# Order of ScalarE's and VectorE's work in RWKV's r stage, and the send of X by column halves, in a six-layer model on one core

## What is computed

```python
r, k, v = rkv[:, :, 0], rkv[:, :, 1], rkv[:, :, 2]
kk = heads(k * k_k)
kk = kk * lax.rsqrt(jnp.maximum(jnp.sum(kk * kk, axis=-1, keepdims=True), 1e-24))
k = k.astype(f32) * (1.0 + (a - 1.0) * k_a)

def step(state, inp):
    r_t, w_t, k_t, v_t, kk_t, a_t = inp
    sa = jnp.einsum('bhvk,bhk->bhv', state, kk_t)
    state = (state * w_t[:, :, None, :]
             - sa[..., None] * (kk_t * a_t)[:, :, None, :]
             + v_t[..., None] * k_t[:, :, None, :])
    return state, jnp.einsum('bhvk,bhk->bhv', state, r_t)
```

```python
y = jnp.einsum('bse,ed->bsd', jnp.concatenate([o_a, o_b], axis=-1), w_out)
y = rms_norm_2(y, post_g)
return x + gate[:, None, :] * y
```

## Time and profile before

| | |
|---|---|
| median of 3 runs | 2015.63 us (2000.81 to 2020.76) |
| the profiled execution | 2018.37 us |
| its span in the profile | 2016.6 us |
| TensorE busy | 1871.5 us (93%) |
| VectorE busy | 1301.9 us (65%) |
| ScalarE busy | 1037.8 us (51%) |
| GpSimd busy | 167.2 us (8%) |
| chain that ended last, on TensorE | 84% |
| mean granted clock | 0.957 |

### The profile page before, as it was taken

One profiled execution on the slowest core, in us unless ns is written; L12 is line 12 of the kernel. 1 busy time (PEld: TensorE's weight loads), 2 busy tenths in 40 slices (PEclk: granted clock), 3 DMA queues, 4 the chain that ended last, 5 costly groups with the idle time before them and its releaser, 6 DMA issues.

```text
span 2016.6 us, 43368 instructions
## 1 busy us (share of the span) xinstructions
PE 1871.5 (93%) x18631; PEld 1653.5 (82%) x18631; DVE 1301.9 (65%) x1838; ACT 1037.8 (51%) x1571; POOL 167.2 (8%) x124
## 2 busy tenths in 40 slices
PE   6988899999899999899799998987999999997997
PEld 6877698899767988898588887877778888886886
DVE  7775367855543777557657766777267765775764
ACT  5744365554333655445465544934365544564454
POOL 0051000000010000012100000042000000001000
PEclk8999999999887999999899999999989999997998
DMA  6320245556653555444547563320055555442541
GB/s 186 126 79 4 65 150 193 186 187 195 208 168 105 188 189 178 147 156 151 184 138 208 193 193 120 105 78 25 4 167 184 192 178 165 144 134 93 162 128 61
DMA packets 288262, 288.16 MB, mean 143 GB/s; under 512 B 15224, under 2 KB 286312, under 8 KB 288072
## 3 DMA queue, kind: packets, MB, share of 16 engines
q1 hardware_dynamic: 284776, 284.28, 44.2%
q10 hardware_dynamic: 3296, 1.11, 0.3%
HBM read 284.32 MB, written 1.05 MB: 142 GB/s over the span
## 4 chain that ended last, share of the span: by engine, by line
PE 84%; DVE 6%; issue 4%; ACT 4%; DMA 1%; POOL 0%; SPq 0%; DVEq 0%; ACTq 0%; POOLq 0%
PE ps L409 21%; PE ps L410 11%; PE ps L391 9%; PE ps L392 9%; PE ps L393 9%; PE ps L783 2%; PE ps L427 2%; PE ps L426 2%; PE ps L428 2%; PE ps L753 1%; PE ps L681 1%; ACT wh L443 1%; DVE wl L453 1%; PE ps L767 1%; PE ps L696 1%
## 5 line engine op out<-in xcount | busy, mean ns | idle before, releaser
L453 DVE TENSOR_TENSOR wl<-raw,wh 128x1024 fp32r<-128x1024 f32 x484 | 596.6, 1249 | 342.6 <-ACT wh L443 337.0
L443 ACT ACTIVATE wh<-raw 128x1024 fp32r<-128x1024 f32 x484 | 500.3, 1042 | 434.5 <-PE ps L410 197.2
L409 PE MATMUL ps<-HH,wh 128*128 128x512 f32 x1408 | 489.3, 391 | 0.0
L410 PE MATMUL ps<-HH,wl 128*128 128x256 f32 x1408 | 397.0, 282 | 0.0
L409 PEld LDWEIGHTS ps<-HH,wh 128*128 128x128 f32 x1408 | 264.3, 188 | 55.3
L391 PE MATMUL ps<-HH,wh 128*128 128x256 f32 x928 | 271.2, 292 | 12.8 <-DVE HH L2414 6.7
L410 PEld LDWEIGHTS ps<-HH,wl 128*128 128x128 f32 x1408 | 266.1, 189 | 0.1
L392 PE MATMUL ps<-HH,wh 128*128 128x256 f32 x928 | 263.6, 284 | 0.0
L393 PE MATMUL ps<-HH,wl 128*128 128x256 f32 x928 | 263.4, 284 | 0.0
L391 PEld LDWEIGHTS ps<-HH,wh 128*128 128x128 f32 x928 | 179.2, 193 | 23.5 <-issue 7.4
L391 PE MATMUL ps<-XH,wh 128*128 128x256 f32 x576 | 168.3, 292 | 16.0 <-DVE XH L1970 16.0
(11 more groups left out here) (328 smaller groups left out, 3256.0 us busy)
## 6 DMA issues: line engine op xcount, KB each, us to landing
raw<-in_ffn_w_gu_dram SPq DMA_DIRECT2D x88, 1024.0 KB, 5.1
raw<-in_ffn_w_down_dram SPq DMA_DIRECT2D x32, 1024.0 KB, 5.3
raw<-in_w_in_dram SPq DMA_DIRECT2D x32, 1024.0 KB, 5.5
raw<-in_rw_w_rkv_dram SPq DMA_DIRECT2D x24, 1024.0 KB, 5.9
B<-in_w_ada_dram SPq DMA_DIRECT2D x24, 1024.0 KB, 7.3
raw<-in_ds_w_in_dram SPq DMA_DIRECT2D x14, 1024.0 KB, 5.0
raw<-in_ffn_w_down_dram SPq DMA_DIRECT2D x16, 768.0 KB, 4.6
raw<-in_sb_w_qkv_dram SPq DMA_DIRECT2D x12, 1024.0 KB, 5.2
```

The source lines that it names most:

```text
L409: e.matmul(o[:, m, :], h_[:, k, c], x_, start=k0 + k == 0, stop=False, skip_group_check=True)
L410: i = e.matmul(o[:, m, 0:S], l_[:, k, c], x_[:, 0, :], start=False, stop=k0 + k == kt - 1, skip_group_check=True)
L443: e.activation(wh[:, u % UNITS, 0:kn * 256], raw[:, j % RAW, k0 * 256:(k0 + kn) * 256], ACT.Copy).then_inc(*up("hi"))
L453: e.tensor_tensor(wl[:, u % UNITS, 0:kn * 256], raw[:, j % RAW, k0 * 256:(k0 + kn) * 256], wh[:, u % UNITS, 0:kn * 256].bitcast(F32), ALU. ...
```

## The change

Three edits.

- The r stage of both RWKV layers. ScalarE now takes a key norm and one group's rounding of v's input in turn, four times; then come the change of table and both exponentials; the two weight roundings and the eviction of r's first block follow behind these. VectorE's two pairs of rests stand behind `erase_and_write(0)` and `erase_and_write(1)`, no longer ahead of them.
- At the end of both hybrid layers VectorE scales group g + 1 before it adds group g, and an addition waits for its own group's scaling alone.
- The last barrier is gone. TensorE's transposes are grouped by feature group, both token halves of one in one bank, and each waits for its own group of X; ScalarE copies a bank at once; SyncE sends columns 0 to 511 after the second copy and columns 512 to 1023 after the fourth.

```diff
@@ sync_program
-            e.wait_ge(*at("act", "x out"))
-            e.dma_start(out_ap.rearrange("a (j p) c -> p (a j) c", p=P), TM(0)).then_inc(s_out, 16)
-            e.wait_ge(s_out, 16)
+            for a in range(2):
+                c = slice(512 * a, 512 * a + 512)
+                e.wait_ge(*at("act", ("end", 2 * a + 1)))
+                e.dma_start(out_ap.rearrange("a (j p) c -> p (a j) c", p=P)[:, :, c], TM(0)[:, :, c]).then_inc(s_out, 16)
+            e.wait_ge(s_out, 32)
@@ tensor_program
-            barrier(e, "mm", "end")
-            for g in range(2):
+            for g in range(4):
+                o = bank(e, ("end", g), ("act", ("end", g)))
+                e.wait_ge(*at("dve", ("y", 1, g)))
                 for j in range(2):
-                    o = bank(e, ("end", g, j), ("act", ("end", g, j)))
-                    for u in range(4):
-                        i = e.transpose(o[:, u * P:u * P + P], X[:, 4 * g + u, j * P:j * P + P], ident)
-                    i.then_inc(*up("mm", ("end", g, j)))
+                    for u in range(2):
+                        i = e.transpose(o[:, (2 * j + u) * P:(2 * j + u) * P + P], X[:, 2 * g + u, j * P:j * P + P], ident)
+                i.then_inc(*up("mm", ("end", g)))
@@ act_rwkv
-            for g in range(3):
+            for g in range(4):
                 key_norm(g)
-            prepare(2, HH, ("unit", ("full", n, 1, 3)))
-            hi(e)
-            evac(0, 0, R_)
-            key_norm(3)
+                rounded(2, HH, g, ("unit", ("full", n, 1, 3)))
             log_and_exp(e)
             key_norm_exp(0)
             key_norm_exp(1)
+            hi(e)
+            evac(0, 0, R_)
@@ dve_rwkv
-            lo(e)
             erase_and_write(0)
             lo(e)
             erase_and_write(1)
+            lo(e)
@@ dve_hybrid
-            for g in range(4):
+
+            def y_normed(g):
                 for k in (2 * g, 2 * g + 1):
                     i = e.scalar_tensor_tensor(out=y[:, k, :], in0=y[:, k, :], scalar=gp[:, k:k + 1], in1=rstd[:, :], op0=ALU.mult, op1=ALU.mult)
-                i.then_inc(*up("dve"))
+                i.then_inc(*up("dve", (L, "yn", g)))
+
+            y_normed(0)
+            for g in range(4):
+                if g < 3:
+                    y_normed(g + 1)
                 xs = X[:, 2 * g:2 * g + 2, :]
-                e.wait_ge(*now("dve"))
+                e.wait_ge(*at("dve", (L, "yn", g)))
                 e.tensor_tensor(xs, xs, y[:, 2 * g:2 * g + 2, :], ALU.add).then_inc(*up("dve", ("y", layer, g)))
```

More of the change, by code:

```diff
@@ L1420, in act_rwkv, with rounded, prepare @@
             R_, k_, v_, cum, a_, vmix, kk, sq = FM(4), FM(5), FM(13), FM(7), FM(8), FM(14), FM(9), FM(6)
-            def prepare(m, hi_, *free):
+            def rounded(m, hi_, g, *free):
+                for ev in free:
+                    e.wait_ge(*at(*ev))
+                e.wait_ge(*at("dve", ("xm", n, m, g)))
+                e.activation(pair(hi_, g), mix_slot(g), ACT.Copy).then_inc(*up("act", ("xmh", n, m, g)))
+            def prepare(m, hi_):
                 for g in range(4):
[L1424 to L1427, removed]
+                    rounded(m, hi_, g)
             def evac(m, g, dst):
@@ L1878, in scalar_program @@
             act_hybrid(e, 1)
-            barrier(e, "act", "end")
             xo = TM(0)
[L1881 to L1884, removed]
+            for g in range(4):
+                e.wait_ge(*at("mm", ("end", g)))
+                e.activation(xo[:, :, g * 256:g * 256 + 256], PS("end", g)[:, :].rearrange("p (j c) -> p j c", j=2),
+                             ACT.Copy).then_inc(*up("act", ("end", g)))
         MX, NM, SM, RS = ([small[:, o + 8 * i:o + 2 + 8 * i] for i in range(4)] + [small[:, z:z + 2]]
@@ L2650, in vector_program @@
             dve_hybrid(e, 1)
-            barrier(e, "dve", "end")
         def pool_square(e, tag):
@@ L2757, in gpsimd_program @@
             pool_hybrid(e, 1)
-            barrier(e, "pool", "end")
         def begin(rehearsal):
```

## The result

| | before | after |
|---|---|---|
| median of 20 runs | 2005.42 us (1999.56 to 2021.12, and one of 2350.37) | 1995.07 us (1990.42 to 2008.5) |
| ratio | | 0.9945 (95% interval 0.9927 to 0.9963) |
| span of the profiled execution | 2016.6 us | 1992.3 us |

The ratio leaves out the one slow run of 2350.37 us. It is worth 11 us of 2005, with 7.4 to 14.6 us inside the interval. The forecast was a gain of 10.4 us. It was put under the median of three runs, 2015.63; twenty runs of the kernel before have a median 10 us lower, 2005.42. The changed kernel came out at 1995.07, under the low end of the range, 1996. It is faster, by less than 1%.

A forecast was written before the change was run, and what follows sets the result against it. TensorE was taken to bound the kernel; 3.4 (layer 0) + 3.1 (layer 3) + 4.2 (tail) - 0.3 (hybrid layer 0) = 10.4 us gained, giving 2008.0 profiled, 2005.2 at the runs' median, stated as 2006 us; range 1996 to 2014.

The forecast's parts named there:

- It lies 2.7 us over the median of the runs, 2015.63; that gives 2005.2: Whole kernel: forecast 2008.0 us for the profiled execution, lowered by 2.7 us to the level of the three runs' median.
- case c: Whole kernel: half-clock spells do not come up again at their shifted places, 10 us more gained, 1995 us; chance 0.13.
- ScalarE: RWKV r stage: ScalarE no longer waits between roundings, and the exponentials start near 77.3 instead of 82.06.
- VectorE: RWKV r stage: key halves start near 78.4, the second is ready at 90.3 instead of 95.2, TensorE's wait gone.
- the 1.2 us: r stage, layer 0: margin by which the rests of r's third group come before TensorE wants them, thinnest in the change.
- the data are there at 96.6, and the rest shifts by 3.4 us: Layer 0's grams: after an instruction refill the work resumes at 96.6 instead of 99.98, gaining 3.4 us, bounds 2.2 to 4.5.
- case (b): r stage: late rests or longer refills leave each layer 0 to 1 us; 5 us gained in all, 2011 us; chance 0.13.
- rival (a): Layer 0's grams: TensorE's clock falls to half after the new stop, costing 12 us; 1.6 us slower, 2017; chance 0.10.
- 84 records in a microsecond: Layer 0's grams: full-clock rate taken from layer 3, used to put the refill boundary, record 100, at 93.1 us.
- Layer 3: Layer 3's grams: VectorE wait of 3.10 us removed, first refill stop grows from 1.21 to 2.0 us, gain 3.1 us.
- The end: Last 15 us: earlier transposes by group give 2.95 us, the halved last send 1.3 us; 4.2 us in all, 2.8 to 5.0.
- If VectorE is first, nothing is lost: End of hybrid layer 0: GpSimd's first sum meets VectorE's third; 0.6 us lost if GpSimd is first; 0.3 us taken.

## Why the prediction was right or wrong

**The level, which put the time outside the range.** The step that failed is "It lies 2.7 us over the median of the runs, 2015.63; that gives 2005.2". Three runs were taken as the level, although they spread over 20 us. Twenty runs gave 2005.42. The forecast gain of 10.4 us taken off that is 1995.0, and 1995.07 was measured. Luck had a part in it: beside the experiments the same kernel's medians were 2010.79, 2012.32 and 2008.99 us, and the changed kernel's, in its second set of runs, was 1998.14, inside the range. The prediction did name half-clock stretches as the thing that moves a run by 12 us (case c, and the earlier trace rows), but it did not ask whether the execution profiled before, with a stretch of 24 us at 0.51, was one of the long ones, and whether three runs could give the level. Its range is also added up wrongly at one end: with the lowest bound of each term, 2.2, 2.3, 2.8 and -0.7, the least gain is 6.6 us, not 7.4.

**ScalarE.** Right in each step: exponentials near 77.3 (77.22), no wait between the roundings.

**VectorE.** Right: first half at 78.4 (78.40), second ready at 90.3 (90.31), the third block's rests in time, no wait of TensorE on either. The experiment with VectorE's order alone showed what stood behind the 1.2 us: 3.6 and 3.7 us of wait in the two layers, and the clock besides.

**Layer 0.** The step that failed is "the data are there at 96.6, and the rest shifts by 3.4 us". The boundary and the record of the stop were right (227, and the added matmuls moved it as that reading says). The length was not: 2.51 instead of 2.0 us, because the load of the next weight piece, which the moved rests now release later, runs beside the fetch. The prediction had seen that loads "now start later fall on the grams", in case (b), and had priced it at nothing in the sum. And the clock fell behind the stop. The sum had the grams at full clock; rival (a) had named a fall at this very place, and held layer 3's example against it. Of the 3.4 us, 0.8 were left in the profiled execution; in six other executions with the same r stage it was 0.6, 1.0, 1.2, 2.2, 2.2 and 2.6, the last three being those in which the clock stayed. A smaller error is the rate: the prediction reads 84 records in a microsecond as 84 records a microsecond, but that count takes in records that only overlap it; 160 records in 2.56 us are 63 a microsecond, which puts the boundary some 0.3 us later.

**Layer 3.** Right: 3.1 forecast, 3.0 measured, 3.0 to 3.3 in four of the other executions, and 1.5 and 1.2 in two, which have a half-clock stretch there. Its first stop was 1.49 instead of 2.0 us.

**The end.** Right: 4.2 forecast, 4.0 measured; 2.8 of it (2.95) by groups and 1.3 (1.3) by the smaller last transfer. The fit that the prediction quotes from the Trainium skill (DMA: Bandwidth & Descriptors, Anatomy of one DMA) is given there for transfers that GpSimd issues; SyncE issued these, and only the rate entered the estimate of 1.2 us.

**Hybrid layer 0.** Near in size, 0.5 us lost where 0.3 were forecast, but not in mechanism. The step that failed is "If VectorE is first, nothing is lost": VectorE's addition was first, by 0.03 us, and GpSimd's sum took 2.39 us instead of 1.26. It is GpSimd that gives way here, not the other way round.

**The sum.** Its terms measured 0.8 + 3.0 + 4.0 - 0.5 = 7.3 us in the trace, where 10.4 were forecast; the ratio says 11. That the forecast and the ratio meet is luck, and not to the credit of the sum. The rest came with a higher mean clock. Over 68 and 32 runs the mean clock differs by 0.0037, and beside each other on one chip by 0.0027 (0.0004 to 0.0050), of which the shorter end explains 0.001. So it is likely, but not shown clear of noise, that the changed kernel meets fewer or shorter half-clock stretches; why the stretches of a stage three layers away should depend on these edits stays open. Case (c) had that sign and was given 0.13.

## What to carry to other kernels

Before a sum is set under a median, look at how runs of one kernel spread and whether time follows the mean granted clock; if it does, one profiled execution is not the level, and a gain under the spread is to be read from distances between the same instructions in both traces. Where a wait is taken out in front of a dense run of small matmuls, ask what TensorE runs into next: here a fetch of instructions, lengthened by a weight load that the same edit had moved onto it, and a fall of the clock behind it took back most of the gain; with that load moved once more, two executions kept all of it. Two reorderings on two engines can be worth nothing and less than nothing apart and be worth it together; price each alone to see which one leans on the other.

## What the runs showed of the hardware

- In dense float32 matmuls of 64x64 TensorE stopped, and where it stopped twice the stops stood 127 records apart (a multiply and a weight load each, 254 instructions). In layer 0's grams the stop was 0.96 and 1.14 us with no weight load beside it, and 2.0 to 2.9 us with one. TensorE went on 1.2 to 1.6 us after the 16 KB transfer of its instructions was done.
- 25 added matmuls, which are 50 records, moved a stop from record 227 to 177.
- In layer 0's grams, behind stops or waits of 2.0 to 2.9 us, the granted clock fell to 0.50 in some executions and stayed at 1.00 in others of the same kernel at the same place (it fell in four of the seven with the changed kernel's r stage). Behind 0.96 and 1.14 us it stayed.
- A send from SBUF took 4.0, 2.7 and 2.1 us from issue to landing for 1024, 512 and 256 KB.
- Where VectorE's additions of two SBUF tensors came first, GpSimd's sum took 2.39 us instead of 1.26; where GpSimd's sum came first, VectorE's addition took 1.73 us instead of 0.69.
